# One state space stage, two halves: Toeplitz blocks spread from chip to chip, or by way of memory

## The reference, cut to what matters

```python
xn = _rmsnorm(h, g_mix)
# 64 groups of 16 channels, each with 64 complex states; ab, bb from lam, log_dt, B
bu = einsum('nlgc,gpc->nlgp', xn, bb)              # complex
h_t = ab * h_{t-1} + bu_t                          # scan over the positions
y = einsum('nlgp,gcp->nlgc', h, c).real + d * xn
z = gelu(y);  gl = z @ w_glu + b_glu;  h = h + gl[:, :1024] * sigmoid(gl[:, 1024:])
```

## Time and profile before

| | |
|---|---|
| median of 3 runs | 1460.81 us (1457.99 to 1462.72) |
| profiled execution | 1463.6 us, of which the span of its instructions is 1461.7 us |
| granted TensorE clock, mean | 0.974 |
| TensorE matmul busy | 1346.2 us, 92% |
| VectorE, ScalarE, POOL busy | 739.9, 441.9, 778.7 us |
| transfers KT from KKE | 64 on SP and 64 on ScalarE, 32 KB each |

### The profile page before, as it was taken

How to read it: one execution, slowest core, us unless ns; L and a number is a source line. 1 busy time by engine, 2 the same in 40 slices (tenths; PEclk the granted TensorE clock), 3 DMA queues, 4 the chain that set the end, 5 groups by cost and what they waited for, 6 DMA issues and landing times.

```text
span 1461.7 us, 28804 instructions
## 1 busy us (share of the span) xinstructions
PE 1346.2 (92%) x10956; PEld 1296.4 (89%) x10956; DVE 739.9 (51%) x1310; ACT 441.9 (30%) x942; POOL 778.7 (53%) x669
## 2 busy tenths in 40 slices
PE   2537689999999999999999988899999999999998
PEld 2436579999999999999999965799999999999997
DVE  6875543345555554123467777455555555212263
ACT  2723221133433432100223257323443433210021
POOL 2690046555666665556565554455666655555552
PEclk9969799999999999999999999999999999999999
DMA  5021233322222223332454320222222223332322
GB/s 107 4 59 30 60 93 97 87 73 87 86 86 86 86 86 107 87 91 78 112 125 112 87 85 13 62 79 87 87 86 86 86 86 91 105 86 80 93 87 65
DMA packets 223526, 120.18 MB, mean 82 GB/s; under 512 B 26221, under 2 KB 220608, under 8 KB 223084
## 3 DMA queue, kind: packets, MB, share of 16 engines
q1 hardware_dynamic: 211320, 104.96, 25.4%
q10 hardware_dynamic: 12140, 14.30, 4.5%
HBM read 110.98 MB, written 6.09 MB: 80 GB/s over the span
## 4 chain that ended last, share of the span: by engine, by line
PE 85%; ACT 5%; ACTq 3%; DVE 3%; SPq 2%; issue 1%; DMA 0%; POOL 0%; DVEq 0%
PE ACC L848 56%; PE MI L848 10%; PE SS L848 9%; PE MI L681 4%; ACTq L1343 3%; SPq L451 2%; PE SS L810 1%; PE SS L805 1%; ACT PB L1663 1%; PE SS L1155 1%; PE ACC L681 1%; ACT XN L1219 1%; DVE PB L2206 1%; PE SS L1033 1%; DVE RSTD L2004 0%
## 5 line engine op out<-in xcount | busy, mean ns | idle before, releaser
L628 POOL TENSOR_TENSOR SPL<-RAW,SPL 128x1024 fp32r<-128x1024 f32 (+2 forms) x172 | 449.8, 2615 | 14.4
L848 PE MATMUL ACC<-NH,SPL 128*128 128x272 f32 x2048 | 350.2, 289 | 0.7 <-DVE AL L2065 0.7
L625 POOL TENSOR_TENSOR TIC<-EPSB 128x1 f32<-128x1 f32 x172 | 36.7, 213 | 570.5 <-PE ACC L848 346.2
L848 PEld LDWEIGHTS ACC<-NH,SPL 128*128 128x128 f32 x2048 | 291.4, 189 | 1.8 <-issue 0.9
L848 PE MATMUL ACC<-AH,SPL 128*128 128x272 f32 x1408 | 237.6, 289 | 0.0
L848 PE MATMUL ACC<-NL,SPL 128*128 128x272 f32 x1024 | 211.3, 288 | 0.0
L848 PEld LDWEIGHTS ACC<-AH,SPL 128*128 128x128 f32 x1408 | 198.9, 188 | 0.2
L626 POOL TENSOR_SCALAR SPL<-RAW 128x1024 fp32r<-128x1024 f32 (+2 forms) x172 | 195.2, 1135 | 0.0
L848 PEld LDWEIGHTS ACC<-NL,SPL 128*128 128x128 f32 x1024 | 161.0, 189 | 0.0
L848 PE MATMUL ACC<-AL,SPL 128*128 128x272 f32 x704 | 145.4, 287 | 0.0
L848 PE MATMUL SS<-NH,SPL 128*128 128x272 f32 x704 | 120.7, 288 | 0.0
(11 more groups left out here) (335 smaller groups left out, 1999.6 us busy)
## 6 DMA issues: line engine op xcount, KB each, us to landing
RAW<-in_w_up_dram SPq DMA_DIRECT2D x88, 512.0 KB
RAW<-in_w_down_dram SPq DMA_DIRECT2D x32, 704.0 KB
RAW<-in_w_glu_dram SPq DMA_DIRECT2D x16, 512.0 KB
RAW<-in_w_ple_gate_dram SPq DMA_DIRECT2D x16, 512.0 KB
RAW<-in_w_q_dram SPq DMA_DIRECT2D x16, 256.0 KB
RAW<-in_w_o_dram SPq DMA_DIRECT2D x32, 128.0 KB
KT<-KKE SPq DMA_DIRECT2D x64, 32.0 KB, 2.0
KT<-KKE ACTq DMA_DIRECT2D x64, 32.0 KB, 2.0
```

The lines of the kernel that those rows point to most:

```text
L625: PIN.tensor_tensor(TIC[:], EPSB[:], EPSB[:], ALU.add)
L628: PIN.tensor_tensor(lo, RAW[:, u, 0:kt, :], hi.bitcast(F32), ALU.subtract).then_inc(sem("split_done"), 1)
L848: last = mm(out[:, h, :], SPL[:, u, w, w0 + k, :], x[:, k0 + k, HT * h:HT * h + HT], start=start and k == 0 and n == 0, stop=stop and k == ...
```

## The change

The taps go to memory and come back. `KKE` is written once per half into `bias_rows`, and 8 transfers per half, one per offset j, read 16 partitions x 8 blocks x 2 KB (256 KB) into `KT[h]`. All of them are issued by SP; ScalarE issues none, and `spread_out` is gone. ScalarE's second copy into `KKE` waits for the first write instead of for `kt_in0`. At the start, B is loaded ahead of C and turned ahead of it on TensorE; the mask `MSK` goes behind C with a semaphore of its own; ScalarE copies `GS` and squares four of the eight rows of x before it copies C; TensorE waits for C's copies at its second column of x. On POOL, `BD` is cleared as soon as x has been scaled and turned, ahead of `DEC`.

```diff
-        def spread(h, j, b):
-            return (KT[h][CG * j:CG * j + CG, b].rearrange("p i f c -> p (i f c)"),
-                    KKE[CG * b:CG * b + CG, CH - 1 - j:2 * CH - 1 - j].rearrange("p t f c -> p (t f c)"))
+        TAPS = (2 * CH - 1) * CG * (KC // 2)
+        kernel_rows = [bias_rows.rearrange("h a n -> (h a n)")[P * TAPS * h:P * TAPS * (h + 1)].rearrange(
+            "(b c n) -> c b n", c=CG, n=TAPS) for h in range(2)]
...
-                sp.dma_start(MSK[:], consts[:, C_MSK:C_MSK + CG]).then_inc(sem("const_in"), 16)
...
+            for r, src in enumerate((ssm_b_re, ssm_b_im)):
+                sp.dma_start(BN[:, r], src[0].rearrange("(q a) s c -> q (a s) c", a=2)).then_inc(sem("b_in"), 16)
             for r, src in enumerate((ssm_c_re, ssm_c_im)):
...
-            for r, src in enumerate((ssm_b_re, ssm_b_im)):
-                sp.dma_start(BN[:, r], src[0].rearrange("(q a) s c -> q (a s) c", a=2)).then_inc(sem("b_in"), 16)
+                sp.dma_start(MSK[:], consts[:, C_MSK:C_MSK + CG]).then_inc(sem("mask_in"), 16)
...
                     for h in range(2):
+                        sp.wait_ge(sem("kk_ready"), h + 1)
+                        sp.dma_start(bias_rows.rearrange("h a n -> (h a n)")[P * TAPS * h:P * TAPS * (h + 1)].rearrange("(p n) -> p n", n=TAPS),
+                                     KKE[:].rearrange("p t f c -> p (t f c)")).then_inc(sem("kk_out"), 16)
                         sp.wait_ge(sem("uz_made"), len(XG))
-                        sp.wait_ge(sem("kk_ready"), h + 1)
                         if h:
                             sp.wait_ge(sem("v_made"), KC // 2)
+                        sp.wait_ge(sem("kk_out"), 16 * h + 16)
                         for j in range(CH):
-                            for b in range(4):
-                                sp.dma_start(*spread(h, j, b)).then_inc(sem("kt_in%d" % h), 16)
+                            at0 = CG * (KC // 2) * (CH - 1 - j)
+                            sp.dma_start(KT[h][CG * j:CG * j + CG].rearrange("p b i f c -> p b (i f c)"),
+                                         kernel_rows[h][:, :, at0:at0 + CG * (KC // 2) * CH]).then_inc(sem("kt_in%d" % h), 16)
...
             powers(0)
+            pool.wait_ge(sem("x_scaled"), 2 * CH)
+            pool.wait_ge(sem("x_made"), 2 * KC)
+            PIN.memset(BD[:], 0.0).then_inc(sem("bd_zero"), 1)
...
-            pool.wait_ge(sem("uz_made"), len(XG))
-            PIN.memset(BD[:], 0.0).then_inc(sem("bd_zero"), 1)
             powers(1)
...
-            for r in range(2):
-                act.wait_ge(sem("c_made"), r + 1)
-                copy(CA[:, r, :, 0, :], ACC[:, r, :].rearrange("p (q c) -> p q c", c=CG), scale=1.0 - 2.0 * r).then_inc(sem("c_turned"), 1)
             act.wait_ge(sem("g_made"), 1)
             copy(GS[:], SS[:, 1, :]).then_inc(sem("g_copied"), 1)
...
             for j in range(CH):
+                if j == CH // 2:
+                    for r in range(2):
+                        act.wait_ge(sem("c_made"), r + 1)
+                        copy(CA[:, r, :, 0, :], ACC[:, r, :].rearrange("p (q c) -> p q c", c=CG), scale=1.0 - 2.0 * r).then_inc(sem("c_turned"), 1)
...
                 if h:
-                    act.wait_ge(sem("kt_in0"), 16 * CH * 8)
+                    act.wait_ge(sem("kk_out"), 16)
...
-            def spread_out(h):
-
-                act.wait_ge(sem("uz_made"), len(XG))
-                act.wait_ge(sem("kk_ready"), h + 1)
-                for j in range(CH):
-                    for b in range(4, 8):
-                        act.dma_start(*spread(h, j, b)).then_inc(sem("kt_in%d" % h), 16)
```

More of the change, by code:

```diff
@@ L452, in _ @@
                                      src[0].rearrange("(t q a) c s -> t a q c s", t=4, a=2)[t, a]).then_inc(sem("c_in"), 16)
-            for r, src in enumerate((ssm_b_re, ssm_b_im)):
-                sp.dma_start(BN[:, r], src[0].rearrange("(q a) s c -> q (a s) c", a=2)).then_inc(sem("b_in"), 16)
+            with nc.allow_non_contiguous_dma(reason="64 small elements"):
+                sp.dma_start(MSK[:], consts[:, C_MSK:C_MSK + CG]).then_inc(sem("mask_in"), 16)
             for at0, src in ((V_GMIX, g_mix), (V_GFFN, g_ffn), (V_GPLE, g_ple)):
@@ L491, in stream @@
                     for h in range(2):
+                        sp.wait_ge(sem("kk_ready"), h + 1)
+                        sp.dma_start(bias_rows.rearrange("h a n -> (h a n)")[P * TAPS * h:P * TAPS * (h + 1)].rearrange("(p n) -> p n", n=TAPS),
+                                     KKE[:].rearrange("p t f c -> p (t f c)")).then_inc(sem("kk_out"), 16)
                         sp.wait_ge(sem("uz_made"), len(XG))
-                        sp.wait_ge(sem("kk_ready"), h + 1)
                         if h:
                             sp.wait_ge(sem("v_made"), KC // 2)
+                        sp.wait_ge(sem("kk_out"), 16 * h + 16)
                         for j in range(CH):
-                            for b in range(4):
-                                sp.dma_start(*spread(h, j, b)).then_inc(sem("kt_in%d" % h), 16)
-                    sp.wait_ge(sem("kt_in1"), 16 * CH * 8)
+                            at0 = CG * (KC // 2) * (CH - 1 - j)
+                            sp.dma_start(KT[h][CG * j:CG * j + CG].rearrange("p b i f c -> p b (i f c)"),
+                                         kernel_rows[h][:, :, at0:at0 + CG * (KC // 2) * CH]).then_inc(sem("kt_in%d" % h), 16)
+                    sp.wait_ge(sem("kt_in1"), 16 * CH)
                     turn(0, False)
@@ L681, in turn @@
                 return tr(out, in_, IDN[0:rows, 0:rows])
-            pe.wait_ge(sem("const_in"), 48)
+            pe.wait_ge(sem("const_in"), 32)
             pe.wait_ge(sem("lam_in"), 48)
@@ L689, in _ @@
             mm(SS[:, 1, :], SEL[:], G2[:], start=True, stop=True).then_inc(sem("g_made"), 1)
+            pe.wait_ge(sem("b_in"), 32)
+            for r in range(2):
+                for c in range(CG):
+                    last = tr(ACC[:, 2 + r, PAIRS * c:PAIRS * c + PAIRS], BN[:, r, :, c], IDN[0:PAIRS, 0:PAIRS])
+            last.then_inc(sem("b_made"), 1)
             pe.wait_ge(sem("c_in"), 256)
@@ L694, in _ @@
                 last.then_inc(sem("c_made"), 1)
-            pe.wait_ge(sem("b_in"), 32)
-            for r in range(2):
-                for c in range(CG):
-                    last = tr(ACC[:, 2 + r, PAIRS * c:PAIRS * c + PAIRS], BN[:, r, :, c], IDN[0:PAIRS, 0:PAIRS])
-            last.then_inc(sem("b_made"), 1)
             pe.wait_ge(sem("x_in"), 112)
@@ L704, in _ @@
             pe.wait_ge(sem("xs_zero"), 1)
-            pe.wait_ge(sem("c_turned"), 2)
             for m in range(KC):
                 for jh in range(2):
+                    if m == 1:
+                        pe.wait_ge(sem("c_turned"), 2)
                     if m >= 2:
@@ L795, in outputs @@
                 par = f % 2
-                pe.wait_ge(sem("kt_in%d" % (f // 4)), 16 * CH * 8)
+                pe.wait_ge(sem("kt_in%d" % (f // 4)), 16 * CH)
                 if f:
@@ L1383, in _ @@
             kernels(0, SS[:, 1, :])
-            spread_out(0)
             samples(0)
@@ L1393, in _ @@
                     samples(f + 1)
-                if f == 2:
-                    spread_out(1)
                 if f:
@@ L1897, in _ @@
             link(T(DGV[:], VEC[:, V_D:V_D + KC], VEC[:, V_GMIX:V_GMIX + KC], M_))
-            dve.wait_ge(sem("const_in"), 48)
+            dve.wait_ge(sem("mask_in"), 16)
             T(DG[:], MSK[:].unsqueeze(1).to_broadcast([P, KC, CG]), DGV[:].unsqueeze(2).to_broadcast([P, KC, CG]), M_).then_inc(sem("dg_ready"), 1)
```

## The result

| | before | after |
|---|---|---|
| time, median of the runs | 1461.59 us (1457.99 to 1462.72) | 1442.46 us (1440.85 to 1443.69) |
| profiled execution | 1463.6 us | 1441.52 us |
| mean granted TensorE clock | 0.974 | 0.981 |

The ratio is 0.9873, 95% interval 0.9851 to 0.9894: faster by 1.3%, 19 us, where the forecast was 32 us (1429). The time is that of the first rival, 1443; the reasons are only in part its own.

What follows compares the result with a forecast made beforehand. Only the state space stage, stopped by ScalarE's KT issues, could change; TensorE is busy elsewhere. First half 14.1 (start included) - clock 2.6 + second half 20.8 = 32.3 us gained, so 1429 us, range 1422 to 1443.

Steps and rivals of the forecast that it cites:

- the first rival: Also rival 1: KT reads into 16 partitions take 2.62 us each, late by 4.2 and 10.0 us; 1443 us, chance 0.25.
- the first half: Without ScalarE's issues, outputs(0) waits for h_ready, starting at 101.9 instead of 115.99: 14.1 us gained, the start's 3 included.
- Second half: From inputs(3) to the GLU product, six loop steps of 6.57 us, 39.4 instead of 60.3: gain 20.8 us.
- Eight in a row: 4.2 + 7 x 1.38 = 13.8 us: A half's eight KT reads: first landing after 4.2 us, each further one 1.38 us, from the BIAS load.
- each us above 13.8 is paid in full: At outputs(4), the second half's reads fit with nothing left, so any read time beyond 13.8 us delays it.
- The clock: TensorE, idle before outputs(0), runs that step at 1.2 GHz: 2.6 us charged once, nothing if the clock holds.
- outputs(0) to outputs(1) stays as it is: TensorE's stretch from outputs(0) to outputs(1) keeps its length after the change: 0 us.
- EROT and scan(0): VectorE before outputs(0): EROT ends at 94.3, scan(0) takes 7.5 us beside POOL (bounds 7.1 to 9.2), h_ready at 101.8.
- the BIAS row: A 262 kB load into 16 partitions, 104 GB/s at 0.55 busy, read as 189 GB/s and counted against the first rival.
- s = 3: At the start, squares and B first bring ScalarE's root and what follows 3 us earlier; bounds -0.5 to 4.65.
- BD and DEC: On POOL, BD's earlier fill takes some 0.9 us off the road to KKE, nothing at the end; DEC costs nothing.
- Rivals 2 and 3: 2: reads go one at a time, 1462 or 1480 us, chance 0.05. 3: full front gain and clock, 1424, 0.08.

Runs made afterwards that it cites:

- e1: The changed kernel with every KT read landing in all 128 partitions instead of 16 (taps in wrong order, time only); 1438.73 us, one run.
- e2: The changed kernel with each KT read taken from one unbroken 256 KB stretch of memory, still into 16 partitions (taps wrong); 1441.83 us, one run.
- e7: e4_six_blocks plus 100 unused identity transposes on TensorE, 56 before inputs(1), 44 before outputs(0); 1431.94 us, ratio 0.9814 to the kernel before.
- e10: The changed kernel with GpSimd's earlier order put back: DEC first, BD's zeros after uz_made, then powers(1); 1444.8 us, ratio 0.9889 to the kernel before.
- e8: The changed kernel without GpSimd's powers(1), CA's second half set to zero (outputs wrong, time only); 1436.5 us, one run.
- e11: The changed kernel with fifteen of eighteen turns rows copied to PSUM, so EROT's products read one SBUF operand; 1440.47 us, ratio 0.9849 to the kernel before.
- e4_six_blocks: The changed kernel with the second half's reads split: blocks 0 to 5 after inputs(2), 6 and 7 after inputs(3); 1435.19 us, 0.9821 of before.
- e3_wide: The changed kernel with eight spreading writes per half from 128 partitions, then one 2 MB read into 128 partitions; 1436.35 us, 0.9831 of before.
- e6_sixteen_two_queues: The changed kernel with ScalarE's queue issuing four of the second half's eight reads, each still into 16 partitions; 1437.27 us, one run.

## Why the prediction was partly right

The mechanism of the first half came as forecast: ScalarE's stop went, and outputs(0) then waited for VectorE's EROT and scan(0). The second half's reads and the clock did not, and the gain was little more than half. Up to the GLU product the forecast was 32.3 us and 18.3 came. The 14.0 us missing are three terms:

- **Second half, 7.8 us.** Forecast 39.4 us from inputs(3) to the GLU product, measured 47.2 (127.21 to 174.39). The step that failed is "Eight in a row: 4.2 + 7 x 1.38 = 13.8 us": the first landing was right (4.1 us), the spacing was 2.1 us, not 1.38, T 19.0 and not 13.8. The 1.38 came from one BIAS load alone in its window, read as if 0.55 busy meant that eight would go 1/0.55 times as fast. e1 and e2 show that the landing holds them, as rival 1 had it, at a price between the two (its 2.62 came from the bias_rows write). The rule "each us above 13.8 is paid in full" held: 5.2 us of waiting. That the wait also drops the clock (2.5 us in outputs(4)) was in no sum.
- **The clock, 3.4 us.** Forecast 2.6 once, on outputs(0), and behind it "outputs(0) to outputs(1) stays as it is". Measured up to inputs(3): 6.0 (22.4 against 16.4), 1.6 in outputs(0) and 4.4 in kernels(1) with outputs(1), which the forecast put at nothing. That the charge is the clock's is shown by e7, which takes 16.4 us at 1.00 throughout; why the clock fell the second time is not shown.
- **EROT and scan(0), 2.9 us.** Forecast 23.9 + 7.5, measured 25.3 + 9.0 with GpSimd beside them throughout. scan(0) was within its bounds (7.1 to 9.2); that EROT itself would lengthen when powers(1) starts earlier was left out of the sum (e10, without the earlier start: 23.5). e8 and e11 show the cause and that its whole price is 12 us, 9 of which the kernel before had paid already (23.9 + 7.1 against 22.0).

The price stood in the trace of the kernel before. The window of the earlier trace rows is wider than the load; in the stretch in which the load's packets ran, the same view of the kernel before reads:

```profile
733.30:735.40 2.10, 2.10 (x19) 2.10 (x18) 1.95 (x2) 0.00 (x0) 2.07 (x1) 1.00 0.66 124
```

So one load took 2.1 us at 124 GB/s, and the queue of eight kept to that: 2.1 us each at 121 to 127 GB/s. The share was 0.66 for the one and 1.09 for the eight. It did not tell how much room was left, and dividing by it gave 189 GB/s, a pace that no queue of reads into 16 partitions kept here. For the same reason the BIAS row did not, as the prediction has it, speak against rival 1.

Right: s = 3 (3.05 at EROT; 0.9979 for the start alone, 3.1 us); the write; BD and DEC worth nothing in the total that e10 could tell; the loop's step, 161.18 - 154.61 = 6.57; no loss behind the stage. KT was in time for outputs(0), but not by the forecast margin: the first half's last read was issued at 84.4 and landed 15.7 us later, at 100.1 and not 96.1, and h_ready was late as well. At the forecast h_ready of 101.8 it would have had 1.7 us to spare, not 5.8. Two of the prediction's signs of being wrong came, outputs(4)'s wait and the half clock in more than the first step. Rivals 2 and 3 did not come. That the time is rival 1's 1443 is luck: its 14.2 us were all reads, 4.2 of them in the first half; here the reads cost 5.2 us of waiting and 2.5 of clock behind it, all in the second half, and the rest came from the other two terms.

## What to carry to other kernels

A rate divided by the busy share of the engines is not a limit: one load moved 124 GB/s at 0.66, eight in a row 121 at 1.09. Before multiplying a transfer's price by eight, take it from the stretch in which its own packets ran, and look for a row where many queue up into as few partitions. When a stall is shortened, price what TensorE's clock does behind each gap that is left. And ask of every wait what piece of memory it guards: e4_six_blocks gained 7 us by waiting for three quarters of it.

## What the runs showed of the hardware

- Reads of 256 KB into 16 partitions each ran at 121 to 131 GB/s, from strided rows or one stretch, from one queue or two, and one alone at 124; a read of 16 KB into each of 128 partitions ran at 410 while its packets ran (8.7 us from issue to landing, 2 MB).
- 2 KB rows into or out of all 128 partitions left the DMA engines half idle: 143 and 147 GB/s from one queue, 195 from two, 190 in e3_wide's writes, each at a share of 0.50 to 0.53. Why is open.
- VectorE's 1024-wide product took 1.22 us with one operand in PSUM and up to 2.93 us with both in SBUF, beside the same GpSimd work.
- With the same instructions up to that point the clock in kernels(1) fell to 0.50 in the changed kernel and stayed at 1.00 in e6_sixteen_two_queues, 4.4 us apart. Of the kernels with reads through memory, those in which it stayed all ran on one chip.
